# Streamed activations at a start address of their own in each stage, and conditioning blocks shared evenly over the FFN layers, in a ten-stage fp32r network on one core

## The chip, the cores and the metric

One NeuronCore of one Trainium2 chip runs the whole program in one launch. The metric is the device time of that core in microseconds (us), from the start of an execution to its end; lower is better.

## The reference, cut to what matters

Two blocks are run one after the other on x of 256 tokens by 1024 channels. The first has two layers of feed-forward (FFN), mixer (an SSD scan in layer 0, latent attention in layer 1), FFN. The second has two layers of a mixer and a "PEER" feed-forward over 16,384 experts. Every sublayer is conditioned on a vector c (the second block on a vector of its own) by a shift, a scale and a gate of 1024 values each:

```python
cond = jax.nn.silu(c)
for i in range(DEPTH):
    mod = (cond @ w_mod[i] + b_mod[i]).reshape(-1, N_SUBLAYERS, 3, D_MODEL)
    h = modulate(x, norm_g[i, 0], mod[:, 0, 0], mod[:, 0, 1])
    x = x + FFN_RES_WEIGHT * mod[:, 0, 2][:, None, :] * swiglu(
        h, ffn_w_gate[i, 0], ffn_w_up[i, 0], ffn_w_down[i, 0])
    ...
def modulate(x, g, shift, scale):
    return rms_norm(x, g) * (1.0 + scale[:, None, :]) + shift[:, None, :]
def swiglu(h, w_gate, w_up, w_down):
    return (jax.nn.silu(h @ w_gate) * (h @ w_up)) @ w_down
```

The FFN is 2816 wide. The PEER sublayer multiplies h by 128 blocks of weights "u" (128 experts each), applies a GELU, weights the result by a routing table and multiplies by 128 blocks "v".

## The kernel before, in words

**Stages.** The ten sublayers are stages s = 0 to 9: FFN in 0, 2, 3 and 5, SSD in 1, latent attention in 4, the second block's mixers in 6 and 8, PEER in 7 and 9. Weights arrive as 957 blocks of 128 x 1024 float32 (512 KB), one after the other, on SyncE's queue into `ring` (four slots) or, in some stages, into eight more slots that lie in the arena.

**Products in parts.** To keep float32 precision at the speed of the fp32r type, each weight block w and each activation h is split in two rounded parts, hi and lo, and each product is three matmuls, hi.hi, lo.hi and hi.lo. ScalarE makes a block's hi part in `weights_hi` (L1148), VectorE its lo part in place of the raw block or in `more_lo` (L1643). One block costs 24 matmuls of 128x128 weights by 128x256 streamed activations. `columns_in_parts` (L519) streams `hh` (h_hi) and `h` (h_lo), one kilobyte per partition for each of eight d. `rows_in_parts` (L552) streams a hi and a lo tile of a gated activation, `gat_hi` in `small` and `gat_lo` in `work`. `front` (L531, L532, L545) does the first three blocks of a stage. Two out-projections stream YHI, YLO (L697) and MHI, MLO (L816) from `more_lo` in the same form. Blocks of columns by stage: 44 in each FFN, 49 in stage 1, 7 in stage 4, 18 in stage 6, 16 + 128 in stage 7, 19 in stage 8, 16 + 128 in stage 9. Blocks of rows: 22 in each FFN, 128 in stages 7 and 9. In stages 7 and 9, from u block 70 to 122, small plain-float32 matmuls of the routing table (L1076) stand between the blocks; they stream from `work`, the ones of L898 and L918 (stages 6 and 8) stream from the arena.

**Places.** The allocator starts every tensor at a multiple of 32 bytes; the first one, `line_half`, is at byte 16512 of the partition, a multiple of 128. Its 8 bytes are followed by `ring`, `weights_hi`, the arena and `more_lo`, all at 32 bytes past a multiple of 128; after `line_rest` (8 bytes) come x (byte 180416), h (188608) and hh, all at 64 past one. `work` (215136) and `small` (223328) are at 96 past one. In the compiled program:

| streamed operand | line | bytes past a multiple of 128 |
|---|---|---|
| YHI, YLO, MHI, MLO in `more_lo` | L697, L816 | 32 |
| h_hi in `hh`, h_lo in `h` | L519, L531, L532, L545 | 64 |
| gat_hi in `small`, gat_lo in `work` | L552 | 96 |

**Conditioning.** Stage s needs group s of 24 conditioning blocks (512 KB each). The first 16 come with the stream, the other 224 on GpSimd's queue into a ring of four slots (`mod_loads`, L2181, L2185, L2204, L2212), and each costs VectorE one product with an accumulated sum (`product`, L1571). They are worked on in the FFN stages only, between the splits of the weight blocks: `ffn` calls `products(block)` after each block, which does a share of the stage's blocks equal to the share of 58 steps that are done, ahead of the multiplication `ffn_a` (L1676) or the split `gate_lo` (L1667) that TensorE waits for. `MOD_GROUPS` gives stage 0 groups 1 and 2 with the rest of group 0 (56 blocks), stages 2 and 3 two groups (48 each), and stage 5 three groups, 7 to 9 (72). A slot is loaded again once its product is done.

## Time and profile before

| | |
|---|---|
| median of the runs shown | 3440.86 us (two runs, 3437.95 and 3443.78) |
| the profiled execution's own time | 3437.65 us |
| its span, first to last instruction | 3435.6 us (2.05 us less) |
| mean granted TensorE clock | 0.986 |
| TensorE matmul busy | 3285.2 us, 96% |
| VectorE busy | 2585.1 us, 75% |

A span is cut by stages at the first matmul of line L531 in each: 43.9, 236.0, 545.7, 738.5, 934.3, 1104.1, 1319.2, 1525.5, 2369.3 and 2583.7 us for stages 0 to 9. Matmuls overlap: each is shown as 0.28 us long, but the next one starts after 0.11 to 0.12 us. Their pace is read from how many of them lie in a window that they fill: of the count, 2.4 are cut by the window's edges and are taken off.

### The profile page before, as it was taken

Reading aid. Unit: us, or ns where it says so; the run is one execution under the profiler, and the core shown is the slowest. Engines: PE = TensorE matmul, PEld = TensorE weight load, DVE = VectorE, ACT = ScalarE, POOL = GpSimd, SP = SyncE. Lnnn points to the kernel's source line nnn. Section 1 sums busy time; section 2 is a strip of 40 time slices with the busy share of each in tenths; the row PEclk is TensorE's granted clock in tenths of the full one; section 3 lists DMA queues with packets and bytes.
Section 4 is the critical chain, followed back from the end, with each engine's and each line's share of the span. In section 5 each row is a group of like instructions: output and inputs, shape, how many; then the busy total and the mean of one; then the engine's idle time right before and its main releaser. Section 6 shows DMA issues by size and latency. Waiting matters only on the chain.

```text
span 3435.6 us, 68787 instructions
## 1 busy us (share of the span) xinstructions
PE 3285.2 (96%) x26804; PEld 3142.9 (91%) x26804; DVE 2585.1 (75%) x4576; ACT 1608.5 (47%) x2594; POOL 196.6 (6%) x331
## 2 busy tenths in 40 slices
PE   6999989999999998999999999999899999999998
PEld 5999769999967898889999999998789999999998
DVE  7989667888836896856978867776846977867777
ACT  3456544454445345234454444444415444444454
POOL 1100001111000220200000000000300000000000
PEclk9999999999999999999999999999999999999999
DMA  9965218979613993135765477775215765567775
GB/s 373 370 223 167 71 48 328 341 275 345 245 34 125 383 375 127 33 123 174 230 212 170 167 230 232 238 234 179 74 44 178 231 218 179 166 199 234 236 236 189
DMA packets 246578, 707.46 MB, mean 206 GB/s; under 512 B 27472, under 2 KB 93008, under 8 KB 244928
## 3 DMA queue, kind: packets, MB, share of 16 engines
q1 hardware_dynamic: 212112, 571.64, 48.9%
q0 software_dynamic: 34224, 132.46, 10.3%
q8 instruction: 167, 2.74, 0.3%
q14 instruction: 75, 0.61, 0.1%
HBM read 669.40 MB, written 34.60 MB: 205 GB/s over the span
## 4 chain that ended last, share of the span: by engine, by line
PE 76%; DMA 9%; DVE 8%; ACT 3%; issue 3%; SPq 0%; DVEq 0%; POOL 0%; POOLq 0%; ACTq 0%
PE psum L519 33%; PE psum L552 24%; DMA ring<-stream 6%; PE psum L1076 3%; DMA arena<-mod_weights 3%; PE psum L898 2%; DVE ring L1643 1%; PE psum L1011 1%; PE psum L649 1%; ACT weights_hi L1148 1%; PE psum L918 1%; PE psum L500 1%; DVE arena L1571 1%; PE psum L531 1%; PE psum L532 1%
## 5 line engine op out<-in xcount | busy, mean ns | idle before, releaser
L519 PE MATMUL psum<-hh,weights_hi 128*128 128x256 f32 x4216 | 1201.5, 285 | 29.9 <-DVE arena L1676 9.7
L1148 ACT ACTIVATE weights_hi<-ring 128x1024 fp32r<-128x1024 f32 x711 | 752.7, 1059 | 971.9 <-DMA ring<-stream 912.1
L519 PE MATMUL psum<-h,weights_hi 128*128 128x256 f32 x4216 | 1183.4, 281 | 0.0
L1643 DVE TENSOR_TENSOR ring<-ring,weights_hi 128x1024 fp32r<-128x1024 f32 x711 | 870.2, 1226 | 414.5 <-ACT weights_hi L1148 411.3
L519 PEld LDWEIGHTS psum<-hh,weights_hi 128*128 128x128 f32 x4216 | 798.8, 189 | 39.7 <-DVE ring L1643 14.0
L519 PE MATMUL psum<-hh,ring 128*128 128x256 f32 x2976 | 834.9, 281 | 0.0
L519 PEld LDWEIGHTS psum<-h,weights_hi 128*128 128x128 f32 x4216 | 799.1, 190 | 0.2
L552 PE MATMUL psum<-small,weights_hi 128*128 128x256 f32 x2752 | 767.8, 279 | 9.2 <-DVE work L1667 5.8
L552 PE MATMUL psum<-work,weights_hi 128*128 128x256 f32 x2752 | 763.7, 277 | 0.0
L552 PE MATMUL psum<-small,ring 128*128 128x256 f32 x2304 | 639.5, 278 | 0.0
L519 PEld LDWEIGHTS psum<-hh,ring 128*128 128x128 f32 x2976 | 564.6, 190 | 0.0
L552 PEld LDWEIGHTS psum<-small,weights_hi 128*128 128x128 f32 x2752 | 518.1, 188 | 14.2 <-issue 8.3
L552 PEld LDWEIGHTS psum<-work,weights_hi 128*128 128x128 f32 x2752 | 517.1, 188 | 0.1
L552 PEld LDWEIGHTS psum<-small,ring 128*128 128x128 f32 x2304 | 433.7, 188 | 0.0
L519 PE MATMUL psum<-hh,more_lo 128*128 128x256 f32 x1240 | 346.6, 279 | 0.0
L1643 DVE TENSOR_TENSOR more_lo<-arena,weights_hi 128x1024 fp32r<-128x1024 f32 x214 | 261.0, 1223 | 63.8 <-ACT weights_hi L1148 63.3
L1571 DVE SCALAR_TENSOR_TENSOR arena<-arena 128x1024 f32<-128x1024 f32 x232 | 281.9, 1220 | 13.9 <-DMA arena<-mod_weights 13.7
L1148 ACT ACTIVATE weights_hi<-arena 128x1024 fp32r<-128x1024 f32 x214 | 225.1, 1054 | 112.1 <-PE psum L519 86.0
L519 PEld LDWEIGHTS psum<-hh,more_lo 128*128 128x128 f32 x1240 | 233.8, 189 | 0.0
L2103 DVE TENSOR_SCALAR work<-kept,small 128x128 f32<-128x128 f32 x512 | 142.7, 343 | 81.4 <-PE psum L1076 76.5
L2114 DVE TENSOR_TENSOR work<-work,arena 128x256 f32<-128x256 f32 x256 | 159.7, 625 | 0.0
L2185 POOL DMA_DIRECT2D arena<-mod_weights x208 | 109.8, 528 | 564.4 <-DVE arena L1571 560.9
(410 smaller groups left out, 3897.8 us busy)
## 6 DMA issues: line engine op xcount, KB each, us to landing
ring<-stream SPq DMA_DIRECT2D x735, 512.0 KB, 3.8
arena<-mod_weights POOLq DMA_DIRECT2D x224, 512.0 KB, 6.9
arena<-stream SPq DMA_DIRECT2D x222, 512.0 KB, 6.1
acts<-small SPq DMA_DIRECT2D x256, 128.0 KB, 2.2
work<-acts SPq DMA_DIRECT2D x256, 128.0 KB, 2.8
arena<-cond_rows POOLq DMA_DIRECT2D x3, 1024.0 KB, 7.8
...
```

Source lines behind the costliest of these rows:

```text
L500: mm = pe.matmul(PS[:, 2, 0:T], ones, SQ[:, d, :], start=(d == 0), stop=(d == DT - 1))
L519: mm = pe.matmul(out, lhs[:, d, :], rhs[:, d, :], start=(d == 0 and p == 0), stop=(d == DT - 1 and p == 2))
L531: pe.matmul(out, w[:, d, :], h_hi[:, d, :], start=opens and d == 0, stop=False, skip_group_check=True)
L552: mm = pe.matmul(acc[:, d, :], lhs[:, d, :], rhs, start=False, stop=False, skip_group_check=True)
L898: mm = pe.matmul(PS[:, (4 * st + b) % 8, j * P:(j + 1) * P], lhs[:, c, :], rhs[:, c, :], start=True, stop=True)
L1076: mm = pe.matmul(PS[:, 4 + g % 4, j * P:(j + 1) * P], OHI[:, g % 2, j, :], OHJ[:, g % 2, j, :], start=True, stop=True)
L1148: act.activation(whi[:, NTH[n] % WS, :], raw(n), ACT.Copy).then_inc(sem["block_hi"], 1)
L1571: return dve.scalar_tensor_tensor(PRODUCT[:, m % 2, :], block, 1.0, COND[:, 0 if g < 6 else 1, :], ALU.mult, ALU.mult, accum_out=modc[:, g ...
L1643: dve.tensor_tensor(low(n), raw(n), whi[:, NTH[n] % WS, :].bitcast(F32), ALU.subtract)\
L2103: dve.tensor_scalar(OHI[:, g % 2, j, :], iota, ijg[:, 0, t:t + 1], ijg[:, 2, t:t + 1], ALU.is_equal, ALU.mult)
L2114: dve.tensor_tensor(gat[:, k % 4, :], sil[:, k % 4, :], WALL[:, :, i * 4 + k], ALU.mult).then_inc(sem["pe_gated"], 1)
L2185: pool.dma_start(MODRING[slot], mods[i * MOD_RING + (first + slot + MOD_RING)]).then_inc(mod_full[slot], 16)
```

## The change

Two things change. First, h, hh, work and small become tensors with 32 words (128 bytes) to spare, allocated together behind x, and the streamed operands are views into them that begin `H_AT[s]` words (h_hi, h_lo and the h before them) or `G_AT[s]` words (gat_hi, gat_lo, gat) behind the tensor's start, by the stage s. Their writers and readers on ScalarE and VectorE (L1140, L1619, L1650, L1161, L1478, L1667, L2114, L2118) use the same views. `line_rest` of 8 bytes becomes `behind_weights` of 120. The weights' places stay as they are. `rs` and `rv` move behind the streamed part of `small`. By the allocator's rule x then starts at byte 180512, and h, hh, work and small all at 32 bytes past a multiple of 128. Second, the 224 conditioning blocks of GpSimd's queue are shared over the four FFN stages with 56 in each, so that a group's blocks can lie in two stages.

```diff
-MOD_GROUPS = {0: (1, 2), 2: (3, 4), 3: (5, 6), 5: (7, 8, 9)}
+MOD_STAGES = (0, 2, 3, 5)
+MOD_BLOCKS = (24 * NSUB - 16) // len(MOD_STAGES)
 MOD_RING = 4
+H_AT = (0, 2, 3, 6, 4, 8, 10, 6, 12, 14)
+G_AT = {0: 2, 2: 3, 3: 8, 5: 10, 7: 6, 9: 16}
+LATEST = 32
...
 def mod_first(f):
-    return 24 * (MOD_GROUPS[f][0] - 1) + (8 if f else 0)
-def mod_count(f):
-    return 24 * len(MOD_GROUPS[f]) + (0 if f else 8)
+    return MOD_BLOCKS * MOD_STAGES.index(f)
...
-        sb("line_half", [P, 2])
+        sb("ahead_of_weights", [P, 2])
...
-        sb("line_rest", [P, 2])
+        sb("behind_weights", [P, 30])
         x = sb("x", [P, DT, T])
-        h, (h_lo,) = sb_twice("h", [P, DT, T], [([P, DT, T], F32R)])
-        hh, (h_hi,) = sb_twice("hh", [P, DT, T], [([P, DT, T], F32R)])
+        h_all, (h_round,) = sb_twice("h", [P, DT * T + LATEST], [([P, DT * T + LATEST], F32R)])
+        hh_all, (hh_round,) = sb_twice("hh", [P, DT * T + LATEST], [([P, DT * T + LATEST], F32R)])
+        work_all, (work_round,) = sb_twice("work", [P, 2048 + LATEST], [([P, 2048 + LATEST], F32R)])
+        small_all, (small_round,) = sb_twice("small", [P, 5 * T + LATEST], [([P, 5 * T + LATEST], F32R)])
+        def tiles(whole, at, n):
+            return whole[:, at:at + n * T].rearrange("p (a t) -> p a t", t=T)
+        def h_lo_of(s):
+            return tiles(h_round, H_AT[s], DT)
+        def h_hi_of(s):
+            return tiles(hh_round, H_AT[s], DT)
+        def gat_lo_of(s):
+            return tiles(work_round, 1024 + G_AT[s], 4)
+        def gat_hi_of(s):
+            return tiles(small_round, G_AT[s], 4)
+        h, hh = tiles(h_all, 0, DT), tiles(hh_all, 0, DT)
...
-            def columns_in_parts(out, w, wl):
+            def columns_in_parts(s, out, w, wl):
+                h_hi, h_lo = h_hi_of(s), h_lo_of(s)
...
-                    rows_in_parts(w, wl, gat_hi[:, j % 2, :], gat_lo[:, j % 4, :], j == FT - 1)
+                    rows_in_parts(w, wl, gat_hi_of(s)[:, j % 2, :], gat_lo_of(s)[:, j % 4, :], j == FT - 1)
...
-                g, tile = (m // 24 + MOD_GROUPS[f][0], m % 24) if f else ((m + 16) // 24, (m + 16) % 24)
+                g, tile = (n + 16) // 24, (n + 16) % 24
...
-                    total = mod_count(s)
+                    total = MOD_BLOCKS
```

## Rows read from the trace of the kernel before

**Rows 1.** The page: busy time, slices, chain of waits.
```profile
PE 3285.2 (96%) x26804; PEld 3142.9 (91%) x26804; DVE 2585.1 (75%) x4576; ACT 1608.5 (47%) x2594; POOL 196.6 (6%) x331
...
PE   6999989999999998999999999999899999999998
...
PE 76%; DMA 9%; DVE 8%; ACT 3%; issue 3%; SPq 0%; DVEq 0%; POOL 0%; POOLq 0%; ACTq 0%
```

**Rows 2.** Windows, L816 and then L697 alone (start 32 past).
```profile
core 0: us, PE busy (x) PEld busy (x), PEclk, DMA share, GB/s
1073.00:1093.00 20.00, 20.00 (x169) 20.00 (x168) 1.00 0.50 160
...
520.00:530.00 10.00, 10.00 (x86) 10.00 (x85) 1.00 0.58 192
```

**Rows 3.** Windows, L519 alone (64 past): stages 0, 3, 9; then beside routing, stage 7.
```profile
60.00:160.00 100.00, 100.00 (x860) 100.00 (x859) 1.00 0.99 376
760.00:860.00 100.00, 100.00 (x860) 100.00 (x859) 1.00 0.94 351
...
2650.00:2750.00 100.00, 100.00 (x859) 100.00 (x859) 1.00 0.72 233
1850.00:1950.00 100.00, 79.38 (x621) 74.62 (x619) 1.00 0.50 171
```

**Rows 4.** Windows, L552 alone (96 past): stages 0, 9; then stage 7.
```profile
170.00:225.00 55.00, 55.00 (x488) 55.00 (x487) 1.00 0.69 259
3300.00:3400.00 100.00, 99.85 (x881) 99.65 (x881) 1.00 0.74 240
2300.00:2345.00 45.00, 44.76 (x381) 44.75 (x381) 1.00 0.69 231
...
2003.00:2359.00 356.00, 354.82 (x3059) 352.81 (x3058) 1.00 0.73 234
```

**Rows 5.** Plain-float32 matmuls: by form (L1076, L918), then windows of L898 and L1076.
```profile
L1076 PE MATMUL psum<-work 128*128 128x128 f32 x1024 | 131.5, 275 | 0.5 <-DVE work L2104 0.5
...
L918 PE MATMUL psum<-arena 128*128 128x128 f32 x192 | 21.8, 275 | 0.0
...
1420.00:1440.00 20.00, 20.00 (x182) 20.00 (x181) 1.00 0.01 1
...
1850.00:1950.00 100.00, 30.97 (x242) 29.18 (x243) 1.00 0.50 171
```

**Rows 6.** Windows, all engines: FFN stages 0, 2, 3 and 5 whole.
```profile
core 0: us, PE busy (x) PEld busy (x) DVE busy (x) ACT busy (x) POOL busy (x), PEclk, DMA share, GB/s
43.90:236.00 192.10, 190.47 (x1616) 187.62 (x1616) 172.71 (x258) 91.91 (x132) 27.44 (x52) 1.00 0.87 326
545.70:738.50 192.80, 190.96 (x1616) 187.89 (x1616) 165.01 (x241) 93.56 (x134) 25.31 (x48) 1.00 0.89 330
738.50:934.30 195.80, 192.22 (x1617) 188.87 (x1617) 164.13 (x240) 92.36 (x132) 25.38 (x48) 0.99 0.81 300
1104.10:1319.20 215.10, 198.22 (x1616) 192.46 (x1616) 189.89 (x290) 93.57 (x134) 40.29 (x74) 0.99 0.90 345
```

**Rows 7.** Waits of TensorE in stage 5 (us in total, times, longest).
```profile
PE psum L519 <- DVE arena L1676: 9.5, 8, 4.1
PE psum L552 <- DVE work L1667: 5.8, 5, 3.4
```

**Rows 8.** Lines of VectorE: L1571 in stage 5, then in stage 0.
```profile
L1571 DVE SCALAR_TENSOR_TENSOR arena<-arena 128x1024 f32<-128x1024 f32 x72 | 87.4, 1221 | 13.2 <-DMA arena<-mod_weights 13.1
...
L1571 DVE SCALAR_TENSOR_TENSOR arena<-arena 128x1024 f32<-128x1024 f32 x56 | 68.1, 1218 | 0.0
```

**Rows 9.** Lines by form: VectorE with starts 4 or 8 bytes on (L1701), and in place.
```profile
L1619 DVE SCALAR_TENSOR_TENSOR h<-x,modc,small 128x256 f32<-128x256 f32 x80 | 32.6, 479 | 0.4
...
L1701 DVE SCALAR_TENSOR_TENSOR arena<-psum,cols,arena 128x255 f32<-128x255 f32 x64 | 30.9, 483 | 2.3
L1701 DVE SCALAR_TENSOR_TENSOR arena<-psum,cols,arena 128x254 f32<-128x254 f32 x64 | 30.7, 480 | 8.2 <-ACT arena L1209 7.0
```

**Rows 10.** Waits of TensorE in stage 7.
```profile
PE psum L531 <- ACT hh L1140: 2.7, 2, 1.3
PE psum L519 <- DVE ring L1643: 2.2, 4, 1.0
PE psum L552 <- DVE work L2118: 1.1, 5, 0.2
```

More of the change, by code:

```diff
@@ L293, in build, with h_of, gat_of @@
         sb("arena_high", [P, 128 - 30 - 4 * MORE, 256])
-        sb("line_rest", [P, 2])
+        sb("behind_weights", [P, 30])
         x = sb("x", [P, DT, T])
-        h, (h_lo,) = sb_twice("h", [P, DT, T], [([P, DT, T], F32R)])
-        hh, (h_hi,) = sb_twice("hh", [P, DT, T], [([P, DT, T], F32R)])
+        h_all, (h_round,) = sb_twice("h", [P, DT * T + LATEST], [([P, DT * T + LATEST], F32R)])
[4 more added lines that the diff above has]
+            return whole[:, at:at + n * T].rearrange("p (a t) -> p a t", t=T)
+        def h_of(s):
+            return tiles(h_all, H_AT[s], DT)
+        def h_lo_of(s):
+            return tiles(h_round, H_AT[s], DT)
+        def h_hi_of(s):
+            return tiles(hh_round, H_AT[s], DT)
+        def gat_of(s):
+            return tiles(work_all, 1024 + G_AT[s], 4)
+        def gat_lo_of(s):
[3 more added lines that the diff above has]
+        h, hh = tiles(h_all, 0, DT), tiles(hh_all, 0, DT)
         vfirst = sb("vfirst", [P, 4, T])
@@ L306, in build @@
         omk = sb("one_minus_k_a", [P, 8])
-        work, (_, gat_lo) = sb_twice("work", [P, 2048], [([P, 1024], F32), ([P, 4, T], F32R)])
-        small, (gat_hi, _) = sb_twice("small", [P, 5, T], [([P, 4, T], F32R), ([P, T], F32)])
-        ijg, rs, rv = small[:, 0:3, :], small[:, 3, :], small[:, 4, :]
+        work, ijg = work_all[:, 0:2048], tiles(small_all, 0, 3)
+        rs, rv = (small_all[:, LATEST + i * T:LATEST + (i + 1) * T] for i in (3, 4))
         PS = ctx.enter_context(nc.psum_tensor("psum", [P, 8, 512], F32))
@@ L314, in build @@
         sil = work[:, 0:1024].rearrange("p (b t) -> p b t", b=4)
-        gat = work[:, 1024:2048].rearrange("p (b t) -> p b t", b=4)
         SQ = AR[:, 120:128, :]
@@ L378, in build @@
         MB = flat(h[:, 0:6, :]).rearrange("p (a b) -> p a b", a=2)
-        SFR, OHB = gat_lo[:, 0, :], gat_lo[:, 1, 0:64]
+        SFR, OHB = work_round[:, 1024:1024 + T], work_round[:, 1024 + T:1024 + T + 64]
         ARG_BANKS = (4, 5, 3, 1)
@@ L524, in front @@
                 at = 8 * IN_PARTS.index(s)
+                h_hi, h_lo = h_hi_of(s), h_lo_of(s)
                 blocks = [(parts(FIRST[s] + n), out, opens) for n, (out, opens) in enumerate(outs[0:2])]
@@ L564, in ffn @@
                         w, wl = parts(base + 2 * k + half_)
-                        columns_in_parts(PS[:, k % 2, half_ * T:(half_ + 1) * T], w, wl)
+                        columns_in_parts(s, PS[:, k % 2, half_ * T:(half_ + 1) * T], w, wl)
                 for j in range(FT):
@@ L598, in ssd @@
                             pe.wait_ge(sem["conv_step"], 4 * SSD_X.index(p - 4) + 4)
-                    columns_in_parts(PS[:, p % 4, 0:T], w, wl)
+                    columns_in_parts(1, PS[:, p % 4, 0:T], w, wl)
                     if p == 20:
@@ L707, in mla @@
                         pe.wait_ge(sem["proj_evac"], ev + p - 3)
-                    columns_in_parts(PS[:, p % 4, 0:T], w, wl)
+                    columns_in_parts(4, PS[:, p % 4, 0:T], w, wl)
                 pe.wait_ge(sem["mla_w"], 64)
@@ L824, in rwkv @@
                     pe.wait_ge(sem["proj_evac"], EV["mix_in", l] + p - 1 + PRIME)
-                    columns_in_parts(PS[:, p % 2, 0:T], w, wl)
+                    columns_in_parts(6 + 2 * l, PS[:, p % 2, 0:T], w, wl)
                     if p == L + 2:
@@ L1044, in peer @@
                         pe.wait_ge(sem["proj_evac"], EV["peer_q", l] + n - 3 + PRIME)
-                    columns_in_parts(PS[:, n % 4, 0:T], w, wl)
+                    columns_in_parts(7 + 2 * l, PS[:, n % 4, 0:T], w, wl)
                 pe.wait_ge(sem["proj_evac"], EV["peer_q", l] + 16 + PRIME)
@@ L1069, in peer @@
                         pe.wait_ge(sem["pe_gelu"], NK * l + n - 3)
-                    columns_in_parts(PS[:, n % 4, 0:T], w, wl)
+                    columns_in_parts(7 + 2 * l, PS[:, n % 4, 0:T], w, wl)
                     for g in w_groups(n):
@@ L1084, in value @@
                     pe.wait_ge(sem["gate_lo"], i * 4 + (GATES["uv", l] + k + 1))
-                    rows_in_parts(w, wl, gat_hi[:, k, :], gat_lo[:, k, :], last)
+                    rows_in_parts(w, wl, gat_hi_of(7 + 2 * l)[:, k, :], gat_lo_of(7 + 2 * l)[:, k, :], last)
                 with pe.Fori(0, NK // 4 - 1) as i:
@@ L1160, in gate_hi @@
                     act.wait_ge(sem["ffn_a"], FT * f + j + 1)
-                    act.activation(gat_hi[:, j % 2, :], ATF[:, j, :], ACT.Copy).then_inc(sem["gate_hi"], 1)
+                    act.activation(gat_hi_of((0, 2, 3, 5)[f])[:, j % 2, :], ATF[:, j, :], ACT.Copy).then_inc(sem["gate_hi"], 1)
                 split_hi(base + 3)
@@ L1618, in normed @@
                     g = modc[:, s, 8 + d:9 + d] if s < NSUB else col("lnf", d)
-                    dve.scalar_tensor_tensor(h[:, d, :], x[:, d, :], g, rs[:, :], ALU.mult, ALU.mult)\
+                    to = h_of(s) if s < NSUB else h
+                    dve.scalar_tensor_tensor(to[:, d, :], x[:, d, :], g, rs[:, :], ALU.mult, ALU.mult)\
                        .then_inc(sem["norm_scaled" if s < NSUB else "out_ready"], 1)
@@ L2113, in gated @@
                         dve.wait_ge(sem["block_used"], i * 4 + (v0 + k - 3))
-                    dve.tensor_tensor(gat[:, k % 4, :], sil[:, k % 4, :], WALL[:, :, i * 4 + k], ALU.mult).then_inc(sem["pe_gated"], 1)
+                    dve.tensor_tensor(gat_of(7 + 2 * l)[:, k % 4, :], sil[:, k % 4, :], WALL[:, :, i * 4 + k], ALU.mult).then_inc(sem["pe_gated"], 1)
                 def gate_lo(k, i):
                     dve.wait_ge(sem["gate_hi"], i * 4 + (GATES["uv", l] + k + 1))
-                    dve.tensor_tensor(gat_lo[:, k % 4, :], gat[:, k % 4, :], gat_hi[:, k % 4, :].bitcast(F32), ALU.subtract)\
+                    dve.tensor_tensor(gat_lo_of(7 + 2 * l)[:, k % 4, :], gat_of(7 + 2 * l)[:, k % 4, :],
+                                      gat_hi_of(7 + 2 * l)[:, k % 4, :].bitcast(F32), ALU.subtract)\
                        .then_inc(sem["gate_lo"], 1)
@@ L2178, in mod_loads @@
                     pool.dma_start(flat(COND), cond_d[0:1, :].to_broadcast([P, 2 * D])).then_inc(sem["cond_rows"], 16)
-                first, blocks = mod_first(f), mod_count(f)
+                first, blocks = mod_first(f), MOD_BLOCKS
                 for slot in range(MOD_RING):
```

9 lines of the change are left out of this document (4 added, 5 removed).

## The prediction, made before the change was run

> **What bounds the kernel now.** I read the page first: TensorE is busy 96% of the span and its matmuls are 76% of the chain that ended last [rows 1]. So two things can move the time: the pace at which matmuls follow each other, and the places where TensorE waits.
>
> *The pace.* A window that one line fills gives it: the window's length over the count less 2.4. All have the granted clock 1.00 in their rows, the 2.4 GHz level, and all these matmuls have the same shape, yet they don't run alike. From `more_lo`, 32 bytes past a multiple of 128: 20.00 us / 166.6 = 120.0 ns [rows 2] (L697: 119.6). From h and hh, 64 past: 100.00 / 857.6 = 116.6 ns in stages 0, 3 and 9 [rows 3]. From small and work, 96 past: 55.00 / 485.6 = 113.3 ns [rows 4]. The DMA share was 0.99 in one L519 window and 0.72 in another at the same pace, so traffic is not what sets it. That is a straight line: 3.33 ns less for each 32 bytes further on, 0.104 ns a byte. Plain-float32 matmuls show no such thing: 275 ns of duration from 32 past and from 96 past alike [rows 5].
>
> There is a second pace. In some stretches L552 runs slower from the same place: 44.76 / 378.6 = 118.2 ns [rows 4]. L519 between the routing matmuls of stage 7 does too: those take 20.00 / 179.6 = 111.4 ns each [rows 5], and (100 - 242 x 0.1114) / 621 leaves 117.6 ns [rows 3, 5]. I read it as another way in which weight loads and streams fall into step, with a price that a start of 64 or 96 doesn't change.
>
> *The waits.* The four FFN stages have the same matmuls. They take 192.1, 192.8, 195.8 and 215.1 us [rows 6]. Stage 5, with 72 conditioning blocks, is the long one: TensorE waits there 9.5 us for L1676 and 5.8 us for L1667 [rows 7], both VectorE operations that stand behind products, and VectorE is busy 189.9 of 215.1 us. Its products wait 13.1 us for their loads, which stage 0 with 56 blocks doesn't show at all [rows 8].
>
> **The change, part by part.**
>
> *Conditioning.* Stage 5 loses 16 products of 1.22 us with 0.08 us of accumulator read behind each, 21 us of VectorE, and 16 loads of 0.5 MB. It then has stage 0's load exactly, 56, and the other stages say what that costs: the mean of 192.1, 192.8 and 195.8 is 193.6, so -21.5 us. From below, the two waits alone are 15.3 us; from above, 215.1 - 192.1 = 23.0. Stages 2 and 3 gain 8 products each (10.4 us of VectorE in idle time: 165.0 and 164.1 us busy become 175, where stage 0 has 172.7 in 192.1 without a wait) and 8 loads, 4.2 MB in 193 us, 22 GB/s on 330 and 300; a window of stage 0 carries 376 [rows 3, 6]. I take 0. If that cover fails, they lose what stage 5 loses for each block, 21.5/24 x 8 = 7 us each. Groups end at other blocks, with the same small operations.
>
> *Starts.* By the addresses, h and hh lie 32 + 4 x H_AT past a multiple of 128: 32, 40, 44, 56, 48, 64, 72, 56, 80, 88 for stages 0 to 9 (before: 64). small and work lie at 40, 44, 64, 72, 56, 96 for stages 0, 2, 3, 5, 7, 9 (before: 96). All are inside the range that the trace shows at its ends and middle, so I interpolate. No row has a start between, so the ends are steps of 32 bytes, rounded down or up (below).
> - Columns, blocks x 24 x the change in ns: stage 0 1056 x 3.33 = +3.5; 1 1176 x 2.5 = +2.9; 2 1056 x 2.08 = +2.2; 3 1056 x 0.83 = +0.9; 4 168 x 1.67 = +0.3; 5 nothing; 6 432 x -0.83 = -0.4; 8 456 x -1.67 = -0.8. In stages 7 and 9 the 53 blocks beside routing (1272 matmuls) already run at 117.6 and I leave them; the other 2184 give +1.8 and, at -2.5 ns, -5.5. Sum +4.9 us.
> - Rows, 528 matmuls in an FFN: stage 0 5.83 ns, +3.1; 2 5.42, +2.9; 3 3.33, +1.8; 5 2.5, +1.3 (on the stage as it is once its waits are gone). Stage 7: mean 354.82 / 3056.6 = 116.1 ns, between the fast 113.6 (99.85 / 878.6) and the slow 118.2 [rows 4], so about 46% or 1413 of 3072 are fast; 56 past costs these 4.17 ns, +5.9. Stage 9 stays at 96: 0. Sum +15.0 us.
>
> TensorE hardly waits in stage 7, some 6 us of 844 [rows 10], so nothing hides a slower matmul there, and other engines have slack. In stage 1, where some waits are, a part of +2.9 may be hidden.
>
> A rule of the Trainium skill speaks against this whole part. Its page "TensorE: Matmul & The Clock Gate", section "Wait — 56ns, not 53.3ns?", puts the start-to-start time of warm matmuls at N / 2.4 GHz + 2.5 ns, with no word of the address: 109.2 ns for 256 columns. The trace disagrees with that number at all three places [rows 2 to 4]; by it the starts would be worth nothing.
>
> *Other engines.* VectorE and ScalarE now write and read h, small and work at starts that are multiples of 4 or 8 bytes only. L1701 does so before, 483 and 480 ns against 479 for L1619 at a multiple of 32 [rows 9]: 0. If it cost something it would be 22 + 22 operations a FFN on engines with slack. The plain matmuls that read `work` don't feel their start [rows 5]: 0.
>
> Sum: 4.9 + 15.0 - 21.5 = -1.6 us on the profiled execution's 3437.65, which is 3.2 us below the median of the runs shown. On the median: 3439 us.
>
> **The rivals.**
> - *Starts count in whole steps of 32 bytes, rounded down.* Then 40 to 56 is as slow as 32: columns +15.0 for stages 0 to 4, +7.3 and +3.1 in stage 7; rows 7.0 + 3.5 in the FFNs and, in stage 7, 1413 x 6.67 + 1659 x 1.8 = 12.4. +48 in place of +20: 3467 us. For it: all rows are multiples of 32 and can't tell. Against: nothing.
> - *Rounded up.* Columns 3.5 - 1.4 - 1.5 - 7.3 = -6.7, rows 1.8 x 3 + 4.7 = +10.1; net -18: 3423 us.
> - *The start plays no part*; the three paces belong to the three lines' patterns (one accumulator over 24 matmuls, a new one after three). For it: each pace occurs on lines of its own only. Against: L816 and L697 have L552's pattern of accumulators or L519's of streams, and neither's pace; and three exact steps of 3.33 ns would be chance. Only conditioning counts: -21.5, 3419 us. This is also what the skill's rule gives.
> - *Starts off the grid of 32 bytes cost more than any on it*, the case on the slower side. 11,256 column and 4,656 row matmuls, 15,912, get such a start. If each paid once more the whole difference seen between places, 6.7 ns, it is +106 us: 3545 us. It crosses 2% from 70 / 15,912 = 4.4 ns each. For it: a start that is no multiple of 32 is new to the streams. Against: VectorE pays nothing [rows 9].
> - *The tensors lie elsewhere*, on a multiple of 128, as 2 + 30 words would have it if nothing were rounded. Starts are then 0 to 56, and on the same line every one is 3.33 ns worse: 21,624 matmuls, less the slow ones, about +60: 3500 us. The addresses speak against it.
> - *Stages 2 and 3 fall behind their loads*: +14, 3453 us. For it: both stages' slices carry over 400 GB/s at their heaviest, as stage 5's do.
> - *Starts off the grid free the streams* of what they share with the weights, which stay at 32: at the best pace seen, 111.4 ns [rows 5], 15,912 x about 4.5 ns = -72 more, 3367 us. Little speaks for it.
>
> **How the numbers follow.** 2% of this kernel is 69 us, about what a measurement can tell from no change for certain. Chances: the forecast as worked out (3428 to 3450) 0.44, rounded down 0.13, rounded up 0.10, no part 0.14, stages 2 and 3 late 0.08, off the grid dearer 0.06, elsewhere 0.02, off the grid freer 0.03. The range 3412 to 3475 holds the first five with their bounds. Slower by over 2% has the dearer grid and the other base, 0.07; faster by over 2% only the last, 0.03; within 2% 0.90.
>
> **What would show it.** In the profile after: stage 5 about 195 us from one first L531 to the next, its waits for L1676 and L1667 gone; stages 2 and 3 no longer than 199. L519's pace in windows: about 120.0 in stage 0, 118.8 in stage 2, 117.5 in 3, 114.2 in 9 ahead of the routing; L552's 119.2 in stage 0, 116.7 in 3, 117.5 or more in stage 7 and 113.3 in 9; L816 still 120.0. The same L519 pace in all stages proves the third rival; equal paces in stages 0 to 4 the first; a pace above 121 ns the fourth. Stage 2, at 44 bytes past, the only start that is no multiple of 8, is where a grid of 8 bytes would show.

## The result and the profile after

The changed kernel takes 3472.84 us, the median of two runs (3472.58 and 3473.09), where the kernel before takes 3440.86. The ratio, with its 95% interval, is 1.0095 [1.0078, 1.0113]; here and below a quotient of the two medians can differ from the ratio given by up to 0.0007. I had forecast 3439, no change. It is 32 us slower. That lies inside the range of 3412 to 3475, but well outside what I gave as the likeliest case (3428 to 3450).

The page of the changed kernel, its busy times and its chain of waits:

```profile
PE 3340.0 (96%) x26804; PEld 3202.8 (92%) x26804; DVE 2584.6 (74%) x4576; ACT 1608.5 (46%) x2594; POOL 197.6 (6%) x331
...
PE 87%; DVE 5%; DMA 4%; ACT 2%; issue 1%; SPq 0%; POOL 0%; DVEq 0%; ACTq 0%; POOLq 0%
```

TensorE has the same 26,804 matmuls as in [rows 1] and 54.8 us more of busy time, and its matmuls went from 76% to 87% of the chain that ended last. VectorE's and ScalarE's times did not move. So the loss is in how the matmuls follow each other.

The four FFN stages of the changed kernel as windows over all engines (columns as in [rows 6]: us, then busy time and count of PE, PEld, DVE, ACT and POOL, granted clock, DMA share, GB/s):

```profile
43.80:238.60 194.80, 193.32 (x1616) 190.46 (x1616) 172.81 (x258) 91.98 (x132) 27.44 (x52) 1.00 0.86 322
551.40:746.10 194.70, 192.92 (x1616) 189.82 (x1616) 173.24 (x257) 93.37 (x134) 29.55 (x56) 1.00 0.91 348
746.10:946.80 200.70, 197.44 (x1616) 194.58 (x1616) 172.72 (x256) 92.21 (x132) 29.58 (x56) 1.00 0.84 310
1119.40:1316.50 197.10, 195.19 (x1617) 191.89 (x1617) 173.64 (x258) 93.63 (x134) 31.83 (x58) 1.00 0.88 334
```

TensorE's waits in stage 5 of the changed kernel (us in total, times, longest), to be held against [rows 7]:

```profile
PE psum L558 <- ACT hh L1166: 2.7, 2, 1.3
PE psum L545 <- DVE arena L1703: 0.2, 1, 0.2
PE psum L525 <- ACT arena L1158: 0.2, 1, 0.2
```

L1703 is the old L1676, L1694 the old L1667. The first waits 0.2 us in place of 9.5, and the second is no longer listed. Stage 5 went from 215.1 to 197.1 us. That part came as forecast. The other nine stages grew, by 2.7, 3.0, 2.0, 5.0, 2.8, 1.9, 22.5, 1.6 and 12.1 us for stages 0 to 4 and 6 to 9: 53.6 us, less 18.0 in stage 5, is the 35.5 us by which the spans differ (3471.1 less 3435.6).

Windows of the changed kernel by line, all read as in [rows 2 to 4]: L545 (columns) alone in stages 0, 3 and 9; L579 (rows) alone in stages 7 and 9; L843 (the old L816).

```profile
60.00:160.00 100.00, 100.00 (x860) 100.00 (x859) 1.00 0.99 376
770.00:860.00 90.00, 90.00 (x746) 90.00 (x745) 1.00 0.98 361
2690.00:2790.00 100.00, 100.00 (x836) 100.00 (x835) 1.00 0.70 229
...
2060.00:2160.00 100.00, 100.00 (x833) 99.90 (x832) 1.00 0.69 226
3300.00:3400.00 100.00, 100.00 (x851) 99.93 (x850) 1.00 0.71 232
...
1087.00:1107.00 20.00, 20.00 (x169) 20.00 (x169) 1.00 0.47 158
```

The first line gives 100.00 / 857.6 = 116.6 ns in stage 0, where the columns now start 32 bytes past a multiple of 128 and I had forecast 120.0. The second gives 121.0 ns in stage 3, 56 past, forecast 117.5. The third gives 120.0 ns in stage 9, 88 past, forecast 114.2. All at the granted clock 1.00, with DMA shares of 0.98 and 0.70 at nearly one pace. The straight line through 32, 64 and 96 is not met at any of the three. L843, whose operands did not move, is at 120.0 as before.

Below, "pace" is the mean distance between the starts of consecutive matmuls of one line in one stage, with the pauses of over 160 ns left out. It agrees with the windows (116.7, 121.1 and 120.1 ns for the three above) and can be had for every stage:

| stage | columns: start, forecast, measured | rows: start, forecast, measured |
|---|---|---|
| 0 | 32, 120.0, 116.7 | 40, 119.2, 118.4 |
| 1 | 40, 119.2, 121.6 | |
| 2 | 44, 118.8, 117.5 | 44, 118.8, 115.7 |
| 3 | 56, 117.5, 121.1 | 64, 116.7, 117.8 |
| 4 | 48, 118.3, 117.9 | |
| 5 | 64, 116.7, 118.4 | 72, 115.8, 117.8 |
| 6 | 72, 115.8, 120.0 | |
| 7 | 56, 117.5, 120.8 | 56, 117.5, 120.2 |
| 8 | 80, 115.0, 117.5 | |
| 9 | 88, 114.2, 120.1 | 96, 113.3, 117.8 |

Two of these need more than a bent line. Columns in stage 5 and rows in stage 9 start exactly where they did before (64 and 96), and still went from 116.7 to 118.4 ns and from a mean of 114.5 to 117.8. Something beside the start past 128 had changed.

### The profile page after: what moved, and what is told of

Read it like the earlier page. It is cut to its first block, busy times and chain, and to the rows that moved or that the text cites. A ratio compares the mean times of both kernels' runs of the same rounds, so it can differ in the third digit from the quotient of the medians.

```text
span 3471.1 us, 68787 instructions
## 1 busy us (share of the span) xinstructions
PE 3340.0 (96%) x26804; PEld 3202.8 (92%) x26804; DVE 2584.6 (74%) x4576; ACT 1608.5 (46%) x2594; POOL 197.6 (6%) x331
## 4 chain that ended last, share of the span: by engine, by line
PE 87%; DVE 5%; DMA 4%; ACT 2%; issue 1%; SPq 0%; POOL 0%; DVEq 0%; ACTq 0%; POOLq 0%
PE psum L545 39%; PE psum L579 28%; PE psum L1103 3%; DMA ring<-stream 2%; PE psum L925 2%; PE psum L1038 1%; PE psum L676 1%; PE psum L945 1%; PE psum L525 1%; DVE ring L1670 1%; PE psum L558 1%; PE psum L559 1%; ACT weights_hi L1174 1%; DVE arena L1728 1%; PE psum L760 1%
## 5 line engine op out<-in xcount | busy, mean ns | idle before, releaser
L545 PE MATMUL psum<-hh,weights_hi 128*128 128x256 f32 x4216 | 1206.9, 286 | 19.1 <-ACT arena L1388 10.5
L545 PE MATMUL psum<-h,weights_hi 128*128 128x256 f32 x4216 | 1190.6, 282 | 0.0
L545 PE MATMUL psum<-hh,ring 128*128 128x256 f32 x2976 | 843.8, 284 | 0.0
L545 PEld LDWEIGHTS psum<-hh,weights_hi 128*128 128x128 f32 x4216 | 803.8, 191 | 25.6 <-issue 13.2
L545 PEld LDWEIGHTS psum<-h,weights_hi 128*128 128x128 f32 x4216 | 804.0, 191 | 0.2
L579 PE MATMUL psum<-small,weights_hi 128*128 128x256 f32 x2752 | 774.2, 281 | 0.4 <-DVE ring L1670 0.4
L579 PE MATMUL psum<-work,weights_hi 128*128 128x256 f32 x2752 | 772.2, 281 | 0.0
L579 PE MATMUL psum<-small,ring 128*128 128x256 f32 x2304 | 649.8, 282 | 0.0
L545 PEld LDWEIGHTS psum<-hh,ring 128*128 128x128 f32 x2976 | 564.1, 190 | 0.0
L579 PEld LDWEIGHTS psum<-small,weights_hi 128*128 128x128 f32 x2752 | 519.9, 189 | 2.1 <-DVE work L2145 0.6
L579 PEld LDWEIGHTS psum<-work,weights_hi 128*128 128x128 f32 x2752 | 519.3, 189 | 0.1
L579 PEld LDWEIGHTS psum<-small,ring 128*128 128x128 f32 x2304 | 434.8, 189 | 0.0
L545 PE MATMUL psum<-hh,more_lo 128*128 128x256 f32 x1240 | 349.0, 281 | 0.0
L545 PEld LDWEIGHTS psum<-hh,more_lo 128*128 128x128 f32 x1240 | 233.9, 189 | 0.0
```

Source lines behind the costliest of these rows:

```text
L545: mm = pe.matmul(out, lhs[:, d, :], rhs[:, d, :], start=(d == 0 and p == 0), stop=(d == DT - 1 and p == 2))
L579: mm = pe.matmul(acc[:, d, :], lhs[:, d, :], rhs, start=False, stop=False, skip_group_check=True)
```

## The experiments

**Which part of the change does what.** One kernel with each part, and the first of them a second time on another occasion.

e1_even_only, the kernel before with only the conditioning shared evenly:

```diff
-MOD_GROUPS = {0: (1, 2), 2: (3, 4), 3: (5, 6), 5: (7, 8, 9)}
+MOD_STAGES = (0, 2, 3, 5)
+MOD_BLOCKS = (24 * NSUB - 16) // len(MOD_STAGES)
...
-    return 24 * (MOD_GROUPS[f][0] - 1) + (8 if f else 0)
+    return MOD_BLOCKS * MOD_STAGES.index(f)
```

> The kernel before with 56 conditioning blocks in each FFN stage and nothing moved. The two parts are additive: stage 5 falls from 215.1 us to about 197 as it did in the changed kernel, the other stages stay within 1 us of before, and the whole is 18 us (0.5%) faster than before, 3423. Rival, that stages 2 and 3 now fall behind their loads and that this is a part of the loss: stages 2 and 3 longer than 192.8 and 195.8 by over 2 us each, the whole no more than 12 us faster. Paces of L519 116.7 and of L552 113.3 ns in all FFN stages, stage 5's rows too.

Measured: 3421.91 us, ratio 0.9933 [0.9907, 0.9958]. Its FFN stages (columns as above):

```profile
43.90:238.30 194.40, 192.86 (x1617) 190.00 (x1617) 172.89 (x258) 91.97 (x132) 27.46 (x52) 1.00 0.86 322
547.50:740.40 192.90, 190.94 (x1617) 187.84 (x1617) 173.04 (x257) 93.71 (x134) 29.55 (x56) 1.00 0.92 352
740.40:936.00 195.60, 192.17 (x1617) 188.78 (x1617) 172.16 (x256) 92.27 (x132) 29.61 (x56) 0.99 0.85 322
1105.70:1299.90 194.20, 192.09 (x1617) 188.80 (x1617) 173.76 (x258) 93.75 (x134) 31.85 (x58) 1.00 0.88 340
```

Stage 5 is at 194.2, 20.9 us less. Stages 2 and 3 are at 192.9 and 195.6 where they were at 192.8 and 195.8, with VectorE up from 165.0 and 164.1 to 173.0 and 172.2 us: the eight blocks more cost them nothing. Not all of the expectation held: the profiled execution is the slowest of the four (3434.70), stage 0 takes 194.4 us with its rows at 117.8 ns in place of 113.3, and stages 7 and 8 take 8.0 and 5.7 us more than before, stage 7 with its rows at 116.9 in place of 115.0. That the same addresses can have two paces is taken up with e11_even_again.

e2_starts_only, the changed kernel with `MOD_GROUPS` and `mod_count` as before:

```diff
-MOD_STAGES = (0, 2, 3, 5)
-MOD_BLOCKS = (24 * NSUB - 16) // len(MOD_STAGES)
+MOD_GROUPS = {0: (1, 2), 2: (3, 4), 3: (5, 6), 5: (7, 8, 9)}
```

> The changed kernel with the old grouping of the conditioning (56, 48, 48, 72). If the starts alone cost what the changed kernel lost plus what stage 5 gained, 32 + 18 = 50 us slower than before, 3491 (1.5%), with the same pace in each stage as in the changed kernel (121.6 in stage 1, 121.1 in 3, 120.8 and 120.2 in 7). Rival, that the slower pace hides a part of stage 5's waits: stage 5 below 215 us and the whole under 3485.

Measured: 3487.74 us, ratio 1.0129 [1.0107, 1.0151], 44.7 us over the kernel before on the same chip (3443.08). Stage 5 is at 215.8 us, and outside it every pace is within 0.4 ns of the changed kernel's. The whole loss comes with the first part of the change, the starts and the room made for them.

e11_even_again is e1_even_only once more, with the same diff, beside the later experiments.

> The even conditioning alone again, beside the one before on the same chip: 0.5% faster than before, with stages 7 and 9 drawing their share of 113.3 and 117.8 anew in each run, so that single runs differ by up to 20 us.

Measured: 3418.79 us, ratio 0.9937 [0.9919, 0.9956]. Its six runs lie within 6.1 us, where the four of e1_even_only spread over 23. One kernel, but its paces in stage 0 are not those of e1_even_only. The windows of L549 (rows) from 172 to 227 us, first of e1_even_only:

```profile
172.00:227.00 55.00, 55.00 (x469) 55.00 (x468) 1.00 0.68 254
```

and of e11_even_again:

```profile
172.00:227.00 55.00, 55.00 (x488) 55.00 (x487) 1.00 0.69 256
```

55.00 / 466.6 = 117.9 ns in one execution, 55.00 / 485.6 = 113.3 in the other. The columns of the same stage went the other way, from 116.7 to 117.8. So columns and rows from the place of before have two paces each, and which one holds changes from one execution to the next. Those of the rows are the two of stage 7 in [rows 4].

**What changed beside the start past 128.** By the compiled program's addresses: before, the hi and the lo stream of a product lie 8192 bytes apart (`hh` and `h`) or 4096 (`small` and the part of `work` that holds gat_lo), both multiples of 256. With 128 bytes to spare in each tensor they lie 8320 and 4224 apart: half of 256 more. And the distance from the weights to the streams changed with every start, since the weights stayed.

e3_hi_lo_apart keeps every start past 128 of before, and moves only the hi streams 128 bytes further from the lo ones (on the base of e1_even_only; all kernels below share the conditioning evenly):

```diff
         h, (h_lo,) = sb_twice("h", [P, DT, T], [([P, DT, T], F32R)])
+        sb("apart", [P, 32])
         hh, (h_hi,) = sb_twice("hh", [P, DT, T], [([P, DT, T], F32R)])
...
+        sb("back", [P, 96])
         work, (_, gat_lo) = sb_twice("work", [P, 2048], [([P, 1024], F32), ([P, 4, T], F32R)])
+        sb("apart_too", [P, 32])
```

> Even conditioning, and all starts at before's 64 and 96 past a multiple of 128, but the hi operand 128 bytes further on in SBUF, so that hi and lo lie 8320 and 4224 bytes apart in place of 8192 and 4096, as in the changed kernel. Theory D (the distance between hi and lo counts, modulo 256 or more): the pace changes, L552 from 113.3 to about 117.8 ns as in stage 9 of the changed kernel, L519 from 116.7 to 118.4 as in its stage 5; the whole about 3455. Theory S (only the start past a multiple of 128 counts, as I predicted): 116.7 and 113.3, the whole 3423 as the even conditioning alone.

Measured: 3449.93 us in one run, 28 over e1_even_only on the same chip. L519 from 60 to 160, then L552 from 172 to 227:

```profile
60.00:160.00 100.00, 100.00 (x847) 100.00 (x846) 1.00 0.99 370
172.00:227.00 55.00, 55.00 (x470) 55.00 (x469) 1.00 0.70 257
```

118.4 and 117.6 ns. By stage the columns are at 118.3 to 118.6, as the changed kernel's in stage 5 (118.4), and the rows at 117.8 (117.0 in stage 2), as its rows in stage 9 (117.8). So the two places that had not moved past a multiple of 128 are reproduced by moving hi alone. Two limits: 117.8 is also the slower of the rows' two paces, and what is new is that it holds through whole stages: here 7 and 9, in the changed kernel and e2_starts_only 9. The kernel before and the even one have means of 114.5 to 116.9 there. And this run can't tell the distance between hi and lo from hi's own distance to the weights, which moved with it.

e4_weights_moved leaves the streams alone and moves the weights' tensors 32 bytes down, on a multiple of 128:

```diff
-        sb("line_half", [P, 2])
         ring, (ring_lo,) = sb_twice("ring", [P, RING, 1024], [([P, RING, 1024], F32R)])
...
-        sb("line_rest", [P, 2])
+        sb("line_rest", [P, 16])
```

> Even conditioning, streamed h, hh, small and work exactly at before's addresses, but all weights (ring, weights_hi, more_lo, arena) 32 bytes lower, at a multiple of 128. Theory S (a streamed operand's own start): L519 116.7 and L552 113.3 as before; L816, whose streams move with the weights from 32 to 0, changes. Theory R (the start relative to the weights that are loaded beside it): L816 stays at 120.0, L519 (now 64 past the weights) takes 113 and L552 (96 past) 110 to 117, anything but unchanged.

Measured: 3449.24 us in one run. L515 (columns) and L548 (rows) in stage 0:

```profile
60.00:160.00 100.00, 100.00 (x851) 100.00 (x850) 1.00 0.99 373
172.00:227.00 55.00, 55.00 (x467) 55.00 (x467) 1.00 0.70 253
```

The columns run at 117.8 ns (before: 116.6) and in short stretches, of stages 1 and 5 among others, at 113.3; the rows at 118.3 to 118.4 in every stage, never at 113.3. L812, the old L816, whose streams moved with the weights, stays at 120.0:

```profile
1083.00:1103.00 20.00, 20.00 (x169) 20.00 (x168) 1.00 0.48 159
```

Not one byte of the h, hh, small and work streams moved. Their start past a multiple of 128 is thus not enough to set the pace: where the weights lie counts too, and the relation of the two fits all three lines. The numbers that I gave for it, 113 and 110 to 117, were still taken from the straight line and missed.

**A map of that relation.** The next three keep hi and lo a multiple of 256 apart by putting h and hh in one tensor, work and small in another (they and those after them, except e8_all_eight_on and e11_even_again, are edits of the changed kernel; smaller shifts of the space between tensors are left out of some diffs).

e5_together, with the starts of the changed kernel:

```diff
-LATEST = 32
+LATEST = 16
-        h_all, (h_round,) = sb_twice("h", [P, DT * T + LATEST], ...)
-        hh_all, (hh_round,) = sb_twice("hh", [P, DT * T + LATEST], ...)
+        h_all, (h_round,) = sb_twice("h", [P, 2 * DT * T + LATEST], ...)
...
-            return tiles(hh_round, H_AT[s], DT)
+            return tiles(h_round, DT * T + H_AT[s], DT)
```

> The changed kernel with its own tables of starts and its even conditioning, but hi and lo 8192 and 4096 bytes apart as in the kernel before; all starts past a multiple of 128 as in the changed kernel. Theory D (the distance of hi and lo is what made it slow): stages at a multiple of 16 return to what the relation to the weights gives, L545's line in stage 5 (32 past the weights) to 116.7 in place of 118.4, the rows of stage 9 (64 past) to 113.3 or 117.8 in turns, but stage 0's columns (0 past) go up from 116.7 to 120.0, as L697. The whole under 3460. Theory G (starts off a grid of 16 bytes are what made it slow): stages 1, 3, 6, 7 (8, 24, 40, 24 past the weights) stay at 120 to 122 and the whole stays at 3465 to 3475.

Measured: 3454.16 us, ratio 1.0046 [1.0030, 1.0063], about half of the changed kernel's loss. Each theory has a part: stages 5 and 9 came back as D says (116.8 and 113.6 ns), while of the starts off a grid of 16 the columns of stages 3 and 7 stay at 120.0 and those of stages 1 and 6 take 118.3 and 119.4, a little under G's mark. L543 from 60 to 160, columns at the weights' own place modulo 256, and L577 (rows, 192 past the weights) from 3300 to 3400:

```profile
60.00:160.00 100.00, 100.00 (x835) 100.00 (x835) 1.00 0.98 363
3300.00:3400.00 100.00, 100.00 (x880) 99.77 (x879) 1.00 0.73 239
```

120.1 ns, the pace of L816 and L697, whose operands also lie at the weights' own place; and 113.9, the rows' good pace of before. This is the run that tells the distance of hi and lo from their places. In stage 0 of the changed kernel hi lay at the weights' place and lo 128 past it, and the columns took 116.7 ns; with both at the weights' place they take 120.0 here, and with both 128 past it 119.0 in stage 6 of the next run. No mean of the two places gives 116.7, so the pair counts.

e6_sweep_upper, the same tensors, with ten other starts for the columns and six for the rows:

```diff
-H_AT = (0, 2, 3, 6, 4, 8, 10, 6, 12, 14)
-G_AT = {0: 2, 2: 3, 3: 8, 5: 10, 7: 6, 9: 16}
+H_AT = (0, 2, 4, 8, 1, 12, 16, 14, 10, 6)
+G_AT = {0: 2, 2: 4, 3: 8, 5: 12, 7: 0, 9: 1}
```

> Hi and lo together, even conditioning, starts 64 to 128 bytes past the weights: columns 64, 72, 80, 96, 68, 112, 128, 120, 104, 88 in stages 0 to 9, rows 72, 80, 96, 112, 64, 68 in stages 0, 2, 3, 5, 7, 9. Theory R (the start relative to the weights, modulo 128): stage 0's columns 113.3 or 117.8, stage 3's columns and rows 118.3, stage 6 (128, that is 0) 120.0. Theory G: 72, 88, 104, 120 all over 119, 80 and 112 not. With the predicted straight line: 112 would be 108 ns.

Measured: 3459.44 us in one run. L544 (columns) in stages 0, 5 and 9, that is 64, 112 and 88 bytes past the weights:

```profile
60.00:160.00 100.00, 100.00 (x852) 100.00 (x851) 1.00 0.99 373
1140.00:1230.00 90.00, 89.47 (x787) 89.17 (x787) 1.00 1.01 394
2690.00:2790.00 100.00, 100.00 (x835) 100.00 (x835) 1.00 0.70 231
```

100.00 / 849.6 = 117.7, 89.47 / 784.6 = 114.0 (113.5 by the starts) and 120.1 ns. The stage at 112 is the find: 113.5 ns for columns over a whole stage. L578 (rows) in stage 5 lies 240 past the weights, the same place modulo 128 only:

```profile
1248.00:1303.00 55.00, 55.00 (x472) 55.00 (x471) 1.00 0.67 249
```

117.1 ns. Theory R, which counted modulo 128, missed twice: stage 6 (128) is at 119.0 and not 120.0, and the columns of stage 3 (96) at 120.0 where the rows, at 224, are at 118.3. G's marks were met on the columns: 72, 88, 104 and 120 lie above 119, 80 and 112 don't.

e7_all_64_past puts all streams 64 past the weights modulo 128, which is 64 for the columns and 192 for the rows modulo 256:

```diff
+H_AT = (0, 0, 0, 0, 0, 0, 0, 0, 0, 0)
+G_AT = {0: 0, 2: 0, 3: 0, 5: 0, 7: 0, 9: 0}
```

> All streamed activations 64 bytes past the weights (96 past a multiple of 128), hi and lo together, even conditioning. Theory R: columns take the two paces of the rows, 113.3 or 117.8 ns, in place of 116.7 or 117.8. If the fast one holds in half of the matmuls the columns gain 13,400 x 1.7 ns = 22 us on the even conditioning alone: 3400, between 3378 (all fast) and 3430 (all slow). Theory S with the line gives 113.3 everywhere and 3378.

Measured: 3424.02 us, ratio 0.9955 [0.9938, 0.9973]. That lies near the slow end of what was expected. Both lines show 117.8 in some stretches and 113.3 in others: columns 117.8 in stages 0, 2 and 3, 114.3 in stage 5, 116.4 in stage 7. In time it is no better than e1_even_only.

The map from these runs, hi and lo a multiple of 256 apart, weights at 32 past a multiple of 128 (in e4_weights_moved at 0):

| streams past the weights, modulo 256 | pace, ns (kernel, line) |
|---|---|
| 0 | 119.8 to 120.0 (L816, L697 in every kernel; e5 columns) |
| 32 | 116.7 or 117.8 (e1, e11 columns) |
| 64 | 113.3 or 117.8 (e4, e6, e7 columns) |
| 96 | 120.0 (e6 columns) |
| 112 | 113.5 (e6 columns); 113.3 in e9 and e12, below |
| 128 | 119.0 (e6 columns of stage 6) |
| 160 | 117.4 (e5 rows) |
| 192 | 113.3 or 117.8 (before, e1, e7, e11 rows) |
| 224 | 118.3 (e4 rows), 118.3 (e6 rows) |
| 240 | 117.2 (e6 rows) |
| 16, 48, 80, 208 | 118.5, 118.4, 118.5, 119.2 |
| 8, 24, 40, 56, 72, 88, 104, 120 | 118.3, 120.0, 119.4, 119.0, 121.3, 120.0, 120.8, 121.2 |
| 136, 152, 168, 200 | 120.1, 120.0, 119.9, 120.0 |
| 12, 140, 68, 196 (no multiples of 8) | 117.5, 116.7, 119.4, 120.0 |

The two entries at 224 come from different addresses, of the weights in one and of the rows in the other, and agree. Most other entries rest on one stage of one execution, so a second pace at them can't be ruled out. No order by distance is to be seen. The twelve odd multiples of 8 all lie at 118.3 to 121.3, but 0, 96 and 208 are as slow, and the odd multiples of 4 (116.7 to 120.0) are no slower than those of 8: the order isn't one of fineness alone.

**Whether it is the relation alone.** e8_all_eight_on moves everything 8 bytes on, weights too, so that all relations are those of e1_even_only:

```diff
-            return ctx.enter_context(nc.sbuf_tensor(name, shape, dt))
+            return ctx.enter_context(nc.sbuf_tensor(name, shape, dt, align_bytes=8))
...
-        sb("line_half", [P, 2])
+        sb("line_half", [P, 16])
```

> Even conditioning and before's relations (columns 32 past the weights, rows 64 past, hi and lo together), but weights, arena, streams and all else 8 bytes further, at 8 past a multiple of 32. Theory R (only the place of the streams relative to the weights counts): L519's line at 116.7 or 117.8, L552's at 113.3 or 117.8, L816's at 120.0, all as before. Theory G (the start itself must lie on a grid of 32 bytes of SBUF): 119 or more on columns and rows alike.

Measured: 3479.16 us in one run (before on that chip 3440.3). L517 and L550 in stage 0:

```profile
60.00:160.00 100.00, 100.00 (x835) 100.00 (x835) 1.00 0.98 366
178.00:233.00 55.00, 55.00 (x461) 55.00 (x460) 1.00 0.65 237
```

120.1 and 119.9 ns. L814, the old L816, is at 120.0, as it was. The relation is not all: off the grid, streams that kept it lose 3.3 and up to 6.7 ns a matmul. The weights left the grid with them, so this run alone can't say which of the two costs it.

e10_streams_eight_on has the weights where e1_even_only has them and only the streams 8 bytes further, at 40 and 200 past the weights (the diff is against e7_all_64_past):

```diff
-H_AT = (0, 0, 0, 0, 0, 0, 0, 0, 0, 0)
+H_AT = (2, 2, 2, 2, 2, 2, 2, 2, 2, 2)
-G_AT = {0: 0, 2: 0, 3: 0, 5: 0, 7: 0, 9: 0}
+G_AT = {0: 2, 2: 2, 3: 2, 5: 2, 7: 2, 9: 2}
...
-        sb("behind_weights", [P, 16])
+        sb("behind_weights", [P, 2])
...
-        sb("gap", [P, 16])
+        sb("gap", [P, 24])
```

> The same absolute starts of the streams (8 past a multiple of 32), with the weights left at a multiple of 32, so 40 and 72 bytes past them. Both theories: columns about 119.4 and rows about 120.0 in every stage, as the sweeps showed at these distances; the whole about 3465 to 3480. If it is fast instead, the sweeps' numbers belong to their stages and not to the starts.

Measured: 3474.4 us in one run; L544 and L578 in stage 0:

```profile
60.00:160.00 100.00, 100.00 (x842) 100.00 (x841) 1.00 0.99 367
177.00:232.00 55.00, 55.00 (x461) 55.00 (x459) 1.00 0.65 232
```

119.1 and 119.9 ns, and the same in all stages (119.2 and 120.0 by the starts), which repeats the map's 40 (119.4) and 200 (120.0). Eight bytes on the streams alone cost nearly as much as eight on both (columns 119.2 against 120.0, rows 120.0 in each).

**A kernel from the map.** e9_columns_112 has all columns at 112 past the weights and leaves the rows at 192 (against e7_all_64_past):

```diff
-H_AT = (0, 0, 0, 0, 0, 0, 0, 0, 0, 0)
+H_AT = (12, 12, 12, 12, 12, 12, 12, 12, 12, 12)
```

> Even conditioning, columns 112 bytes past the weights in all stages, rows 64 past, hi and lo together. If 113.5, as in the one stage of the sweep that had it, holds for all columns, 13,400 x 3.2 ns = 43 us less than the even conditioning alone: 3379. If that stage was merely in the fast one of two paces, as stage 5 was in the run with all at 64, 3400 to 3425.

Measured: 3391.29 us, ratio 0.9860 [0.9836, 0.9885]. The time lies between the two that were expected. Columns are at 113.3 to 113.5 in the FFN stages and 114.1 to 114.6 elsewhere; beside the routing matmuls they are at 115.7. Rows keep their two paces (116.1 in stage 9).

e12_all_112 puts the rows there as well, modulo 256; their starts are 368 past the weights modulo 512, the same place as 112 only if the rule counts modulo 256 or less:

```diff
-G_AT = {0: 0, 2: 0, 3: 0, 5: 0, 7: 0, 9: 0}
+G_AT = {0: 12, 2: 12, 3: 12, 5: 12, 7: 12, 9: 12}
...
-        sb("gap", [P, 16])
+        sb("gap", [P, 48])
```

> As the run with the columns 112 past the weights, with the rows' streams too at 112 past the weights modulo 256 (in the upper sweep the rows of stage 5 stood at 240, which is 112 modulo 128 only, and took 117.2 ns, while columns at 112 took 113.5). Theory M (the relation counts modulo 256): rows 113.3 in every stage and no more draws of 117.8, the whole 10 to 15 us under the 3391 of that run, near 3378. Theory N (modulo 128, and rows differ from columns): rows 117.2, the whole 3391 + 8,256 x 2.5 ns = about 3410.

Measured: 3378.45 us, ratio 0.9826 [0.9813, 0.9839], the fastest of all and ahead of both kernels. L544 in stages 0 and 3, then L578 in stages 0 and 9:

```profile
60.00:160.00 100.00, 100.00 (x885) 100.00 (x884) 1.00 1.00 388
745.00:835.00 90.00, 90.00 (x797) 90.00 (x796) 1.00 1.00 387
...
168.00:223.00 55.00, 55.00 (x488) 55.00 (x487) 1.00 0.68 257
3200.00:3300.00 100.00, 99.89 (x876) 99.35 (x875) 1.00 0.73 238
```

113.3, 113.3 and 113.3 ns; in the last, 99.89 / 873.6 = 114.3 with small pauses. With the 117.1 at 240 in e6_sweep_upper, this speaks for a rule modulo 256. No stage of the profiled execution shows the 117.8 any more (the slowest stretch, the columns beside the routing matmuls, is at 114.9), and the kernel's five runs lie within 5.2 us (3374.86 to 3380.04), where the eleven of the kernel before on one chip spread over 21 (3431.45 to 3452.12). What is next can be read in its chain of waits and in TensorE's longest waits:

```profile
PE 77%; DMA 9%; DVE 7%; ACT 3%; issue 3%; SPq 1%; DVEq 0%; POOL 0%; ACTq 0%; POOLq 0%
...
PE psum L544 <- DVE ring L1669: 14.4, 19, 4.8
```

The columns wait 14.4 us for splits of weights, 19 times, where the kernel before has this line:

```profile
PE psum L519 <- DVE ring L1643: 9.5, 8, 3.1
```

A part of the faster pace is given back there.

## Why the prediction failed, by its steps

**What bounds the kernel** held: TensorE's pace and the waits of stage 5 were the two things that moved.

**Conditioning, -21.5 us**, held. Alone it took 20.9 and 21.8 us off stage 5 (e1_even_only, e11_even_again). In the changed kernel stage 5 lost 18.0, because its matmuls became slower at the same time. Taking 0 for stages 2 and 3 was right, and the rival in which they fall behind their loads (3453) is out: its mechanism did not occur.

**Starts, +19.9 us** (4.9 columns, 15.0 rows), is the step that failed: alone they cost 44.7 us (e2_starts_only). The nine stages other than 5 grew by 53.6 us, and 32 of the 34 us missed lie in stages 7 and 9, where I had +7.7 and -5.5 and where it was +22.5 and +12.1. The failing sentence is "That is a straight line: 3.33 ns less for each 32 bytes further on", and with it "All are inside the range that the trace shows at its ends and middle, so I interpolate". Three points came from three operands that differed in more than the start past 128. By the map they lie 0, 32 and 192 past the weights modulo 256. There the paces are 120.0, 116.7 and 113.3; between the last two, at 96, it is 120.0 again. I wrote that weights "stay at 32" in one rival only, and never asked what the streams' place is relative to.

Inside this step, runs show three things that the pace depends on:
- *The relation to the weights, modulo 256.* e4_weights_moved changed the paces without touching a stream of h, hh, small or work; e9_columns_112 and e12_all_112 were built from it and came out faster.
- *The distance of hi and lo.* Half of 256 more costs 1.7 ns a column, and it holds the rows at 117.8, up to 4.4 ns above their better pace (e3_hi_lo_apart against the 116.7 and 113.3 of before). At the changed kernel's own starts it is 1.0095 against 1.0046, some 17 us. It is in no line of the change's description: it comes from 32 words to spare in each of four tensors. I had the addresses of all four and read them only modulo 128. It isn't a loss everywhere: with the distance back at a multiple of 256 (e5_together) the columns of stage 0 went up from 116.7 to 120.0, the rows of stages 0 and 5 from 118.4 and 117.8 to 120.1 and 119.9. Most of what it cost lies in stage 9, which is 864.0 us long with it and 848.6 without.
- *The fineness of the start.* 40, 56, 72 and 88, the starts of columns in stages 1, 3, 6, 7 and 9 and of rows in 0, 5 and 7, are 8 past a grid of 16. e8_all_eight_on and e10_streams_eight_on show 119.2 to 120.5 ns for such streams at the two pairs of relations that they have, and the map has 118.3 to 121.3 at its twelve. That no start off the grid is good is not shown: 140 past the weights, an odd multiple of 4, has 116.7.

**Second pace.** I took the 118.2 of stage 7 as "another way in which weight loads and streams fall into step, with a price that a start of 64 or 96 doesn't change", and left 1272 matmuls in each of stages 7 and 9 out of the sum. It is 117.8, seen at the relations 32, 64 and 192, where it comes and goes from one execution to the next; at 112 it did not occur in any stage of e12_all_112's trace. So it does depend on the place. The columns beside the routing matmuls, which I left out, went from 117.9 to 120.3 and 120.4 ns: 3 us more in each of the two stages.

**"Nothing hides a slower matmul there"** was wrong as well, and it hid a part of the loss. [rows 10] lists some 6 us of waits, but what TensorE's pauses of over 160 ns in L519 and L552 add beyond the pace is 12.8 us in stage 7 and 18.1 in stage 9 of the kernel before. In L545 and L579 of the changed kernel it is 6.8 and 8.6. So some 15 us of slower matmuls disappeared into pauses that got shorter; e12_all_112, with the fastest matmuls, has 18.4 and 18.7.

**Other engines, 0**, held: VectorE is busy 2584.6 us against 2585.1, and L1646, the old L1619, takes 482 ns against 479 [rows 9]. For the plain-float32 matmuls I had compared durations, which are not a pace; by pace they agree too, 111.4 ns for L1076 before and 111.2 to 111.5 for L1103 after, with `work` 96 and 32 past a multiple of 128.

**The rivals.** "Rounded down" gave 3467, the nearest number, for a wrong reason: L545 in stage 0 would be at 120.0. "Off the grid dearer", to which I gave 0.06, has the right mechanism for much of the loss; my mark for it, a pace above 121 ns, was met in stages 1 and 3 (121.6, 121.1). I had priced it at up to 6.7 ns, and against 116.7 for columns and 113.3 to 117.8 for rows it is 1.6 to 6.7, mostly below the 4.4 at which it would cross 2%. "The start plays no part" (3419) is out: one line, L543, runs at 116.8 to 120.0 ns by stage in one execution of e5_together. "Rounded up" and "off the grid freer" would have made it faster than before. The tensors lie where the prediction put them, so "elsewhere" (3500) is out. Stage 2, at 44, where a grid of 8 bytes was to show, has milder paces (117.5 and 115.7) than the starts that are odd multiples of 8.

Against the estimate of 109.2 ns by the rule that the prediction cites from the Trainium skill, no run came nearer than 113.3. The rule is stated for back-to-back matmuls, and here each has a weight load of its own, so how much of that gap is due to addresses isn't shown. Another page of the Trainium skill, "SBUF — State Buffer", section "A bandwidth-pool intuition that's wrong (but worth ruling out)", gives TensorE a second, independent read port for its weight loads; it says nothing of addresses, but by it I would expect the weights' place to be of no account to the streams. e4_weights_moved disagrees: 32 bytes on the weights took the rows from 113.3 or 117.8 to 118.3 ns.

**Open.** That the weight loads' reads are what the streams meet is an inference. e4_weights_moved moves the weights for their writers too. DMA traffic doesn't set the pace, which is the same at DMA shares of 0.99 and 0.72 [rows 3], but what ScalarE and VectorE write was not varied. It wasn't tried whether weights off the grid cost anything on their own, nor what chooses between 113.3 and 117.8, nor other distances of hi and lo than 0 and 128 modulo 256, nor most of the relations from 128 to 256.
